# A two-block model on one core: masks of group 1, squares, mean square and evacuation of z at other places in the order of units

## The chip, the core and the metric

The program runs on one core of a Trainium2 chip. Its time is the device time of one execution in microseconds (us). TensorE multiplies matrices, VectorE and ScalarE work element by element, GpSimd (POOL in the profile) does a few small operations and issues some transfers, and SyncE (SP) issues nearly all transfers. Each engine works through its own queue in the order in which the program was written; between engines semaphores order the work.

## The reference, cut to what matters

256 tokens of width 2048 go through a state space layer, an attention layer, and a second block (neighbourhood attention and a large MLP). Only the state space layer is touched:

```python
def _mamba2_mixer(x, w_in, conv_w, conv_b, dt_bias, a_log, d_skip, norm_w, w_out):
    zxbcdt = x @ w_in                       # z 4096, xbc 6144, dt 64 columns
    xbc = silu(causal_conv4(xbc) + conv_b)  # xs 4096, B 8x128, C 8x128
    dt = softplus(dt_raw + dt_bias); a = -exp(a_log)
    y = _ssd_chunked(xs, dt, a, bm, cm) + xs * d_skip
    y = y * silu(z)
    yg = y.reshape(bsz, seqlen, 8, 512)
    yg = yg * rsqrt(mean(square(yg), axis=-1) + EPS)
    return (yg.reshape(...) * norm_w) @ w_out

# _ssd_chunked, for each head of a group (8 groups of 8 heads):
#   y[q] = sum over s <= q of (C[q] . B[s]) * exp(cum[q] - cum[s]) * dt[s] * x[s]
```

(`causal_conv4`, `silu`, `mean` and the comments stand for the reference's own longer lines.)

## The kernel before, in words

**Units.** The work of TensorE is a list of units, made by `plan` (from line 93). A unit multiplies one weight tile of 128 x 2048 (1 MB) with the activations. Every weight is split into a high part (`whi`, a copy in fp32r by ScalarE, L1399) and a low part (`wlo`, the rest, by VectorE, L1831), and so are the activations. A feature unit (form A) makes 128 output features for all 256 tokens, in one bank of PSUM: 16 matmuls of 512 columns (L1080) and 16 of 256 (L1084). A token unit (form B) makes 512 features for two tiles of 128 tokens, in two banks, 12 matmuls of 512 columns each (L1101, L1103, L1105). Banks 0 to 3 are taken in turn; a block waits until the one that was there four blocks before is evacuated. Banks 4 to 7, called `side[0]` to `side[3]`, serve all small work; `side_uses` (L651) names for every use which of them it takes, and a use waits until the use before it on that bank is read.

**The state space layer.** Group g has the units B, C, x0 to x3, then zf0 to zf3 (the gate z of that group), and then ao0 to ao3, the product of group g - 1 with the output weights. Group 0 has its z ahead instead and no ao behind it. So the units are 5 to 10 for group 0, 11 to 20 for B, C, x and z of group 1, 21 to 24 the output units of group 0, 25 to 34 group 2, 35 to 38 the output of group 1, and so on; 95 to 104 is group 7, 105 to 108 the output of group 6 and 109 to 112 that of group 7.

**The order within a unit** is written out by `script` (L222). For unit u: `late` of unit u - 1 (evacuation: of a feature unit, ScalarE copies the half with the low parts, L1446 for B, C and x and L1437 for z, and VectorE adds the other half, L1918 and L1899; for B, C and x the convolution follows on VectorE, L1791); `hi` and `lo` (split of the weights of unit u + 2); `post` (silu of unit u - 1 on ScalarE, L1453); what `timetable` put into `first`; the matmuls (of a token unit, the evacuation of its first block comes between its two halves); the load of the weights of unit u + 5; and what `timetable` put into `after`. Each engine runs those parts of this list that it has a part in, in this order.

**The group's own work** is the stage `ssd` with the steps n = 0, 1, 2, ..., one behind each unit from B of the group on (`timetable`, L162). `late = 2` in the names below is an offset for groups 0 and 1. The steps that the change touches or that stand beside them:
- `cb`: C·B for all pairs of tokens (TensorE, L1167 and L1168, into `side[2]`), and then the mask with the triangle on VectorE (L2049, "kcb"), at n = 3, for group 1 at n = 6;
- `px` at n = 7: x of the group transposed (TensorE, L1176, into `side[2]` and `side[3]`), then times dt (VectorE, L2058);
- the differences of the sums for the heads (Relu on ScalarE, L1512 and L1514), `decays`: Exp of them (L1552), times the mask (VectorE, L2066);
- `o` at n = 8 and 9 + late: the heads' products (TensorE, L1197 and L1199, `side[0]` and `side[1]`), then y1, y2 and y3 on VectorE (L2073, L2077, L2080): times exp(cum), plus the skip term (ScalarE, L1538, at n = 8), times silu(z);
- `sq` at n = 10 + late: the squares (ScalarE, L1542) and the high part of y times the norm's weight, `th` (L1546, into A2h);
- at n = 11 + late on VectorE two sums of the squares (L2083, L2085) and the low parts, `tl` (L1791 with A2l);
- `rs` at n = 12 + late: four products with a column of ones (TensorE, L1184, into `side[3]`);
- `ms` at n = 13 + late: scale and epsilon (VectorE, L2095), and the power -0.5 on GpSimd (L2502), which the evacuation of the group's output units needs (`mul_add` with SM);
- on SyncE: `cum_load` at n = 8 + late, the next group's sums broadcast to all partitions (1 MB, L957), and `exp_load` at n = 8, for group 1 at n = 9 (two of 256 KB, L968), behind `rs` of the group before.

The copies of z (L1437) wait until silu(z) of the group before has been used (`y3`, group - 1), since both share `zs`.

Of the kernel before, what the change touches and what calls it, by code (L numbers as in the profile page):

```python
# [16 lines left out]
NG = 8  # L17
# [146 lines left out]
def timetable(units):  # L164
    at = {u[1]: n for n, u in enumerate(units)}
# [7 lines left out]
    for g in range(NG):  # L173
        start = at["B", g]
        run(("ssd", g), start, 16 if g < 2 else 14)
        if g == 3:
            run(("rope",), at["C", 3], 7)
# [46 lines left out]
def script(units):  # L224
# [4 lines left out]
    for u, (form, tag, *_) in enumerate(units):  # L229
        to_pre = u < last and units[u + 1][1] in PRE  # L230
        if u:
            yield ("late", u - 1)
# [136 lines left out]
def stack_kernel(nc, wst, xT, xtok, pos, cols, rows, nabias, consts, out):  # L369
# [7 lines left out]
    with ExitStack() as ctx:  # L377
# [269 lines left out]
        def side_uses(s):  # L647
# [4 lines left out]
            elif what == "ssd":  # L652
                g, n = r
                late = 2 if g < 2 else 0
                if s == ("ssd", 0, 1):
                    yield from ((("zq", i), 2 + i) for i in range(2))
                if n == (6 if g == 1 else 3):
                    yield ("cb", g), 2
                if n == 7:
                    yield from ((("px", g, t), 2 + t) for t in range(NT))  # L660
                if n in (8 + late, 9 + late):
                    yield ("o", g, n - 8 - late), n - 8 - late
                if n == 12 + late:
                    yield ("rs", g), 3
            elif what == "turn":
# [228 lines left out]
        def sync_program(e):  # L894
# [75 lines left out]
            def ssd(g, n):  # L970
                late = 2 if g < 2 else 0
                if n == (9 if g == 1 else 8):
                    exp_load(g)
                if g == 0 and n == 3:
                    cum_load(0)
                if n == 8 + late and g + 1 < NG:
                    cum_load(g + 1)
# [66 lines left out]
        def tensor_program(e):  # L1044
# [106 lines left out]
            def ssd(g, n):  # L1151
                late = 2 if g < 2 else 0
                if g == 0 and n == 1:
                    w.wait_ge(s_ko, 16)
                    for i in range(2):
# [6 lines left out]
                        tr.then_inc(*ssd_p.inc(f"z{i}", 0))  # L1162
                if n == (6 if g == 1 else 3):
                    o = free(("cb", g))
                    w.wait_ge(*conv_a("silu", 6 * g))
                    w.wait_ge(*conv_a("silu", 6 * g + 1))
                    e.matmul(o[:, 0:T], xf[0][:, 0:P], xf[1], start=True, stop=True)  # L1167
                    e.matmul(o[:, T:T + P], xf[0][:, P:T], xf[1][:, P:T], start=True,  # L1168
                             stop=True).then_inc(*ssd_p.inc("cb", g))
# [8 lines left out]
                if n in (8 + late, 9 + late):  # L1178
                    heads_out(g, n - 8 - late)
                if n == 12 + late:  # L1180
                    o = free(("rs", g))
                    w.wait_ge(*ssd_v("a1", g))
                    for t in range(NT):
                        mean = e.matmul(o[:, t:t + 1], ex[:, t * P:(t + 1) * P], tri[:, P:P + 1], start=True, stop=True)  # L1184
                    mean.then_inc(*ssd_p.inc("rs", g))
# [182 lines left out]
        def scalar_program(e):  # L1368
# [133 lines left out]
            def ssd(g, n):  # L1502
# [25 lines left out]
                if n == 8:  # L1528
# [6 lines left out]
                    for f in range(4):  # L1535
# [3 lines left out]
                                     scale=CO[:, c:c + 1]).then_inc(*ssd_a.inc(f"k{f}", g))  # L1539
                if n == 10 + late:  # L1540
                    w.wait_ge(*ssd_v("y3", g))
# [245 lines left out]
        def vector_program(e):  # L1787
# [254 lines left out]
            def ssd(g, n):  # L2042
                late = 2 if g < 2 else 0
                if n == (6 if g == 1 else 3):
                    w.wait_ge(*ssd_p("cb", g))
# [28 lines left out]
                if n == 10 + late:  # L2074
# [5 lines left out]
                    e.tensor_tensor(yf, yf, zs, ALU.mult).then_inc(*ssd_v.inc("y3", g))  # L2080
                if n == 11 + late:
                    w.wait_ge(*ssd_a("sq", g))
# [5 lines left out]
                    for f in range(4):  # L2088
# [3 lines left out]
                                ALU.subtract).then_inc(*ssd_v.inc(f"tl{f}", g))  # L2092
                if n == 13 + late:
                    w.wait_ge(*ssd_p("rs", g))
                    e.tensor_scalar(SM[:, S_T + 2:S_T + 4], side[SIDE["rs", g][0]][:, 0:2], 1.0 / 512, EPS, ALU.mult,  # L2095
                                    ALU.add).then_inc(*ssd_v.inc("ms", g))
# [401 lines left out]
        def gpsimd_program(e):  # L2498
# [5 lines left out]
            def ssd(g, n):  # L2504
                if n == 13 + (2 if g < 2 else 0):
                    w.wait_ge(*ssd_v("ms", g))
# [175 lines left out]
```

## Time and profile before

| | us |
|---|---|
| median of 3 runs (2115.88 to 2117.52) | 2117.29 |
| the profiled execution | 2116.24 |
| its span | 2114.5 |
| TensorE busy (PE) | 2099.0, 99% |
| VectorE busy (DVE) | 1537.8, 73% |
| ScalarE busy (ACT) | 1133.1, 54% |
| GpSimd busy (POOL) | 53.6, 3% |
| mean granted clock of TensorE | 0.998 |

The span is from the first to the last instruction of the profiled execution. Busy times are sums over an engine's instructions; an engine can be busy and late at the same time, and its idle time costs only where TensorE, which ends last, waits for it. Times in the rows below are us from the start of the span, of this one execution. In a timeline a row merges neighbouring instructions of one line (xN is their number), and brackets give the idle time ahead of it and what ended it. PEclk is the granted clock as a share of full speed: 1.00 is 2.4 GHz, 0.50 is 1.2 GHz.

### The profile page before, as it was taken

To read this page: it belongs to the slowest core of one execution; us is meant where nothing else is said; L and a number is where in the kernel's file an instruction comes from. 1 tells how busy PE (TensorE), PEld (TensorE's weight loads), DVE (VectorE), ACT (ScalarE), POOL (GpSimd) and SP (SyncE) were. 2 spreads that over 40 slices of the span, in tenths; PEclk is the share of its full clock that TensorE was granted. 3 is DMA by queue.
4 is the path that set the end of the run, shared out by engine and by line. 5 is a ranking of instruction groups with operands and counts; after the bars stand their busy time and mean duration, and the time that the engine had idled before them with its cause. 6 is when DMAs were issued, how large, how long until landed. Compare 5 with 4: busy or idle time off the path is not lost.

```text
span 2114.5 us, 27498 instructions
## 1 busy us (share of the span) xinstructions
PE 2099.0 (99%) x10886; PEld 1773.8 (84%) x10886; DVE 1537.8 (73%) x2040; ACT 1133.1 (54%) x1411; POOL 53.6 (3%) x42
## 2 busy tenths in 40 slices
PE   9989999999999999999999999999999999999999
PEld 7878888888888888888888888888888888888887
DVE  7778778777778877675675556556778688787775
ACT  6765565665664556663555445544545454455452
POOL 0000000000000000000010111000000000000000
PEclk9999999999999999999999999999999999999999
DMA  8554555556555554445464544455575666556653
GB/s 320 202 201 170 209 187 201 190 194 210 192 199 181 196 192 146 156 142 199 168 241 174 192 173 161 172 184 201 197 239 183 221 211 197 224 186 212 239 177 141
DMA packets 68144, 411.28 MB, mean 195 GB/s; under 512 B 7472, under 2 KB 14384, under 8 KB 20656
## 3 DMA queue, kind: packets, MB, share of 16 engines
q1 hardware_dynamic: 66000, 394.85, 51.6%
q0 software_dynamic: 2016, 14.68, 3.8%
q8 instruction: 86, 1.41, 0.3%
q14 instruction: 42, 0.34, 0.0%
HBM read 407.27 MB, written 2.23 MB: 194 GB/s over the span
## 4 chain that ended last, share of the span: by engine, by line
PE 91%; DVE 2%; ACT 1%; issue 1%; DMA 0%; POOL 0%; SPq 0%; DVEq 0%
PE bank L1080 23%; PE bank L1101 15%; PE bank L1105 14%; PE bank L1103 14%; PE bank L1084 12%; PE bank L1117 2%; PE bank L1119 2%; PE bank L1121 2%; PE bank L1335 1%; DVE wlo L1831 1%; PE bank L1271 1%; PE bank L1197 1%; PE bank L1293 0%; PE bank L1230 0%; PE bank L1323 0%
## 5 line engine op out<-in xcount | busy, mean ns | idle before, releaser
L1831 DVE TENSOR_TENSOR wlo<-raw,whi 128x2048 fp32r<-128x2048 f32 x318 | 727.8, 2289 | 259.0 <-ACT whi L1399 228.7
L1399 ACT ACTIVATE whi<-raw 128x2048 fp32r<-128x2048 f32 x318 | 607.1, 1911 | 262.1 <-PE bank L1105 246.7
L1080 PE MATMUL bank<-A,whi 128*128 128x512 f32 x2448 | 590.7, 394 | 0.0
L1080 PEld LDWEIGHTS bank<-A,whi 128*128 128x128 f32 x2448 | 454.0, 189 | 93.1 <-issue 2.4
L1084 PEld LDWEIGHTS bank<-A,wlo 128*128 128x128 f32 x2448 | 313.9, 191 | 11.9
L1084 PE MATMUL bank<-A,wlo 128*128 128x256 f32 x2448 | 317.4, 283 | 0.0
L1101 PE MATMUL bank<-whi,A2h 128*128 128x512 f32 x800 | 314.2, 393 | 0.0
L1103 PE MATMUL bank<-whi,A2l 128*128 128x512 f32 x800 | 311.7, 390 | 0.0
L1105 PE MATMUL bank<-wlo,A2h 128*128 128x512 f32 x800 | 311.5, 389 | 0.0
L1101 PE MATMUL bank<-whi,A 128*128 128x512 f32 x608 | 241.9, 398 | 0.8 <-ACT whi L1389 0.8
L1105 PE MATMUL bank<-wlo,A 128*128 128x512 f32 x608 | 237.7, 391 | 0.1
L1103 PE MATMUL bank<-whi,A 128*128 128x512 f32 x608 | 237.1, 390 | 0.0
L1101 PEld LDWEIGHTS bank<-whi,A2h 128*128 128x128 f32 x800 | 150.2, 188 | 32.1 <-issue 1.4
L1105 PEld LDWEIGHTS bank<-wlo,A2h 128*128 128x128 f32 x800 | 150.2, 188 | 31.7
L1103 PEld LDWEIGHTS bank<-whi,A2l 128*128 128x128 f32 x800 | 150.3, 188 | 30.4
L1831 DVE TENSOR_TENSOR wlo<-W,whi 128x2048 fp32r<-128x2048 f32 x56 | 128.3, 2291 | 45.4 <-ACT whi L1399 44.6
L1399 ACT ACTIVATE whi<-W 128x2048 fp32r<-128x2048 f32 x56 | 107.0, 1914 | 68.9 <-DVE W L1842 45.7
L1105 PEld LDWEIGHTS bank<-wlo,A 128*128 128x128 f32 x608 | 114.1, 188 | 26.6 <-DVE wlo L1819 2.7
L1101 PEld LDWEIGHTS bank<-whi,A 128*128 128x128 f32 x608 | 114.3, 188 | 25.5 <-issue 1.7
L1103 PEld LDWEIGHTS bank<-whi,A 128*128 128x128 f32 x608 | 114.3, 188 | 23.1 <-DVE A L2208 0.7
L1434 ACT ACTIVATE W<-bank 128x256 f32<-128x256 f32 x60 | 23.0, 384 | 180.4 <-PE bank L1084 180.4
L1791 DVE SCALAR_TENSOR_TENSOR XR<-bank,SM,XR 128x512 f32<-128x512 f32 x110 | 80.8, 746 | 16.4 <-PE bank L1105 16.3
(262 smaller groups left out, 1831.4 us busy)
## 6 DMA issues: line engine op xcount, KB each, us to landing
raw<-wst SPq DMA_DIRECT2D x313, 1024.0 KB, 4.8
W<-wst SPq DMA_DIRECT2D x33, 1024.0 KB, 5.0
W<-wst POOLq DMA_DIRECT2D x9, 1024.0 KB, 8.0
W<-cum_scratch SPq DMA_DIRECT2D x8, 1024.0 KB, 8.2
W<-rows SPq DMA_DIRECT2D x21, 256.0 KB, 5.8
raw<-wst POOLq DMA_DIRECT2D x5, 1024.0 KB, 7.9
raw<-wst SPq DMA_DIRECT2D x16, 256.0 KB, 7.3
W<-exp_scratch SPq DMA_DIRECT2D x16, 256.0 KB, 6.4
```

Source lines behind the costliest of these rows:

```text
L1080: e.matmul(o[:, :], whi[:, s, k * P:(k + 1) * P], A1[:, k, :, :].rearrange("p h t -> p (h t)"), start=k == 0, stop=False)
L1084: last = e.matmul(o[:, T:2 * T], wlo[:, s, k * P:(k + 1) * P], A1h[:, k, :], start=False, stop=k == KT - 1)
L1101: e.matmul(o, h, wh, start=opens and k == 0, stop=False)
L1103: e.matmul(o, low, wh, start=False, stop=False)
L1105: last = e.matmul(o, h, wl, start=False, stop=t in shut(tag) and k == 3)
L1117: e.matmul(o, h, wh, start=name in ("a", "b", "d", "f") and k == 0, stop=False)
L1119: e.matmul(o, low, wh, start=False, stop=False)
L1121: last = e.matmul(o, h, wl, start=False, stop=k == 3)
L1399: e.activation(whi[:, u % 3, :], raw_of(u), ACT.Copy).then_inc(*hi.inc((u, 3)))
L1434: e.activation(W[:, M_R + i % 4 * T:M_R + (i % 4 + 1) * T], rest, ACT.Copy).then_inc(*rest_a.inc(u))
L1791: return e.scalar_tensor_tensor(out=o, in0=a, scalar=s, in1=b, op0=op0, op1=op1)
L1831: e.tensor_tensor(wlo[:, u % 3, :], raw_of(u), whi[:, u % 3, :], ALU.subtract).then_inc(*lo.inc((u, 3)))
```

## The change

The stage `ssd` keeps its operations and sizes; their places in the list move.
- Group 1's `cb` (products and masks) is at n = 4 instead of 6, that is after unit 15 instead of after unit 17.
- For all groups, squares and `th` are at 11 + late (before 10), the sums and `tl` at 12 + late (11), `rs` at 13 + late (12), `ms` and the power at 14 + late (13): one unit later each. `rs` takes `side[1]` instead of `side[3]`.
- Because of the added step, groups 0 and 7, whose steps fill all units up to their first output unit, get the last one in `first` of that output unit (21 and 109).
- `exp_load` is at n = 10 for group 1 (9) and at n = 6 for all others (8).
- The z units of group 1: `late` of units 17 and 18 is dropped from its place in units 18 and 19 and stands, ahead of `late` of unit 19, at the head of unit 20.

```diff
--- before.py
+++ after.py
@@ -172,7 +172,12 @@
     run(("dt",), at["z", 0, 3], 8)
     for g in range(NG):
         start = at["B", g]
-        run(("ssd", g), start, 16 if g < 2 else 14)
+        if g in (0, NG - 1):
+            steps = at["ao", g, 0] - start
+            run(("ssd", g), start, steps)
+            first[at["ao", g, 0]].append(("ssd", g, steps))
+        else:
+            run(("ssd", g), start, 17 if g == 1 else 15)
         if g == 3:
             run(("rope",), at["C", 3], 7)
     q0 = at["q", 0, 0]
@@ -228,7 +233,9 @@
     yield ("begin",)
     for u, (form, tag, *_) in enumerate(units):
         to_pre = u < last and units[u + 1][1] in PRE
-        if u:
+        if tag == ("zf", 1, 3):
+            yield from (("late", u - 3), ("late", u - 2))
+        if u and tag not in (("zf", 1, 1), ("zf", 1, 2)):
             yield ("late", u - 1)
         if tag in PRE:
             r = PRE[tag]
@@ -654,14 +661,14 @@
                 late = 2 if g < 2 else 0
                 if s == ("ssd", 0, 1):
                     yield from ((("zq", i), 2 + i) for i in range(2))
-                if n == (6 if g == 1 else 3):
+                if n == (4 if g == 1 else 3):
                     yield ("cb", g), 2
                 if n == 7:
                     yield from ((("px", g, t), 2 + t) for t in range(NT))
                 if n in (8 + late, 9 + late):
                     yield ("o", g, n - 8 - late), n - 8 - late
-                if n == 12 + late:
-                    yield ("rs", g), 3
+                if n == 13 + late:
+                    yield ("rs", g), 1
             elif what == "turn":
                 yield from ((("turn", r[0], r[1], pr), 2 * r[1] + pr) for pr in range(2))
             elif what == "quarter":
@@ -969,7 +976,7 @@
 
             def ssd(g, n):
                 late = 2 if g < 2 else 0
-                if n == (9 if g == 1 else 8):
+                if n == (10 if g == 1 else 6):
                     exp_load(g)
                 if g == 0 and n == 3:
                     cum_load(0)
@@ -1160,7 +1167,7 @@
                                 tr = e.transpose(o[:, f * T + t * P:f * T + (t + 1) * P],
                                                  z0[t][:, (2 * i + f) * P:(2 * i + f + 1) * P], ident)
                         tr.then_inc(*ssd_p.inc(f"z{i}", 0))
-                if n == (6 if g == 1 else 3):
+                if n == (4 if g == 1 else 3):
                     o = free(("cb", g))
                     w.wait_ge(*conv_a("silu", 6 * g))
                     w.wait_ge(*conv_a("silu", 6 * g + 1))
@@ -1177,7 +1184,7 @@
                     tr.then_inc(*ssd_p.inc("px", g))
                 if n in (8 + late, 9 + late):
                     heads_out(g, n - 8 - late)
-                if n == 12 + late:
+                if n == 13 + late:
                     o = free(("rs", g))
                     w.wait_ge(*ssd_v("a1", g))
                     for t in range(NT):
@@ -1537,7 +1544,7 @@
                         w.wait_ge(*conv_a("silu", 6 * g + 2 + f))
                         e.activation(yf[:, f, :], xf[2 + f], ACT.Identity,
                                      scale=CO[:, c:c + 1]).then_inc(*ssd_a.inc(f"k{f}", g))
-                if n == 10 + late:
+                if n == 11 + late:
                     w.wait_ge(*ssd_v("y3", g))
                     e.activation(ex, y, ACT.Square).then_inc(*ssd_a.inc("sq", g))
                     if g >= 2:
@@ -2041,7 +2048,7 @@
 
             def ssd(g, n):
                 late = 2 if g < 2 else 0
-                if n == (6 if g == 1 else 3):
+                if n == (4 if g == 1 else 3):
                     w.wait_ge(*ssd_p("cb", g))
                     w.wait_ge(s_ko, 16)
                     if g:
@@ -2078,7 +2085,7 @@
                     w.wait_ge(*ssd_v("y2", g))
                     w.wait_ge(*(zs_a("s", g) if g else ssd_a("zs1", 0)))
                     e.tensor_tensor(yf, yf, zs, ALU.mult).then_inc(*ssd_v.inc("y3", g))
-                if n == 11 + late:
+                if n == 12 + late:
                     w.wait_ge(*ssd_a("sq", g))
                     e.tensor_tensor(ex[:, 0:512], ex[:, 0:512], ex[:, 512:1024], ALU.add).then_inc(*ssd_v.inc("a0", g))
                     w.wait_ge(*ssd_v("a0", g))
@@ -2090,7 +2097,7 @@
                         w.wait_ge(*ssd_a(f"th{f}", g))
                         mul_add(A2l[:, kt, :], yf[:, f, :], norm_w(g, f), A2h[:, kt, :], ALU.mult,
                                 ALU.subtract).then_inc(*ssd_v.inc(f"tl{f}", g))
-                if n == 13 + late:
+                if n == 14 + late:
                     w.wait_ge(*ssd_p("rs", g))
                     e.tensor_scalar(SM[:, S_T + 2:S_T + 4], side[SIDE["rs", g][0]][:, 0:2], 1.0 / 512, EPS, ALU.mult,
                                     ALU.add).then_inc(*ssd_v.inc("ms", g))
@@ -2502,7 +2509,7 @@
                 return e.tensor_tensor(SM[:, to:to + n], SM[:, src:src + n], SM[:, S_MH:S_MH + n], ALU.pow)
 
             def ssd(g, n):
-                if n == 13 + (2 if g < 2 else 0):
+                if n == 14 + (2 if g < 2 else 0):
                     w.wait_ge(*ssd_v("ms", g))
                     if g >= 2:
                         w.wait_ge(*evac_v((at["ao", g - 2, ND - 1], 1)))
```

## Rows read from the trace of the kernel before

**Rows 1.** What TensorE waited for, 0 to 700 us: us, times, longest.

```profile
PE bank L1184 <- DVE W L2058: 4.3, 1, 4.3
PE bank L1176 <- DVE W L2049: 3.3, 1, 3.3
PE bank L1184 <- DVE W L2085: 0.7, 1, 0.7
```

**Rows 2.** TensorE's timeline: start us, us, what [idle before <-releaser].

```profile
82.64 1.04 PE L1176 MATMUL bank<-KO,W 128*128 128x128 f32 x8
...
83.43 3.92 PE L1080 MATMUL bank<-A,whi 128*128 128x512 f32 x16
...
124.42 1.52 PE L1176 MATMUL bank<-KO,W 128*128 128x128 f32 x8 [3.30 <-DVE W L2049]
...
137.03 1.02 PE L1184 MATMUL bank<-KO,W 128*128 128x1 f32 x4 [4.34 <-DVE W L2058]
...
145.47 0.40 PE L1101 MATMUL bank<-whi,A2h 128*128 128x512 f32 x1
...
151.03 0.65 PE L1197 MATMUL bank<-W 128*64 128x256 f32 x4
...
158.14 0.65 PE L1197 MATMUL bank<-W 128*64 128x256 f32 x4
```

**Rows 3.** Windows: us, busy of PE, PEld, DVE, ACT, POOL; PEclk; DMA.

```profile
126.00:128.00 2.00, 2.00 (x6) 1.52 (x6) 0.00 (x0) 2.00 (x7) 0.00 (x0) 0.50 0.00 0
...
139.00:141.00 2.00, 2.00 (x6) 1.55 (x5) 2.00 (x2) 2.00 (x7) 0.00 (x0) 0.50 0.07 16
```

**Rows 4.** VectorE's timeline in the same stretch.

```profile
122.68 1.23 DVE L2080 TENSOR_TENSOR W<-W 128x1024 f32<-128x1024 f32 x1
...
123.82 0.55 DVE L2049 TENSOR_TENSOR W<-bank,KO 128x384 f32<-128x384 f32 x1
...
129.03 0.42 DVE L1899 TENSOR_TENSOR W<-bank,W 128x256 f32<-128x256 f32 x1 [4.66 <-ACT W L1437]
...
133.04 0.69 DVE L2083 TENSOR_TENSOR W<-W 128x512 f32<-128x512 f32 x1
...
134.11 1.66 DVE L1791 SCALAR_TENSOR_TENSOR A2l<-W,CO,A2h 128x256 fp32r<-128x256 f32 x4
...
139.42 1.75 DVE L2066 TENSOR_TENSOR W<-W 128x1536 f32<-128x1536 f32 x1
```

**Rows 5.** ScalarE's timeline in the same stretch.

```profile
123.94 1.06 ACT L1542 ACTIVATE W<-W 128x1024 f32<-128x1024 f32 x1 [4.90 <-DVE W L2080]
...
124.90 1.69 ACT L1546 ACTIVATE A2h<-W,CO 128x256 fp32r<-128x256 f32 x4
...
126.50 0.49 ACT L1512 ACTIVATE W<-W 128x256 f32<-128x256 f32 x1
...
128.83 1.90 ACT L1399 ACTIVATE whi<-raw 128x2048 fp32r<-128x2048 f32 x1
...
136.27 1.28 ACT L1552 ACT_TABLE_LOAD   x1
...
138.96 1.69 ACT L1538 ACTIVATE W<-W,CO 128x256 f32<-128x256 f32 x4
...
140.56 0.36 ACT L1437 ACTIVATE W<-bank 128x256 f32<-128x256 f32 x1
```

**Rows 6.** GpSimd's timeline, 100 to 170 us.

```profile
145.34 2.10 POOL L2502 TENSOR_TENSOR SM<-SM 128x2 f32<-128x2 f32 x1 [144.89 <-DVE SM L2095]
```

**Rows 7.** Broadcasts: sums (by tile), wait before L2073, exp (page).

```profile
L957 SPq DMA_DIRECT2D W<-cum_scratch x1: 423/423/423, 111.6 to 111.6; - x1
DMA to landing us min/median/max: 7.0/7.0/7.0
...
  DMA W<-exp_scratch: 17.9, 6
...
W<-exp_scratch SPq DMA_DIRECT2D x16, 256.0 KB, 6.4
```

## The prediction

> **What bounds the kernel now.** The first view is the list of what TensorE waited for: the reader is to see that, apart from startup and the norms, only three rows name the state space layer, 4.3, 3.3 and 0.7 us [rows 1]. TensorE sets the end of this program, so only what it waits for, or does at a lower clock, can be won. The second view is TensorE's timeline around the two long waits [rows 2]. It shows that unit 18 ends at 124.42 - 3.30 = 121.1, that the transposes of x of group 1 then stand for the masks (L2049), that the mean square of group 0 stands from 132.7 to 137.0 for L2058, and that unit 21, the first output unit, opens at 145.47. A whole unit takes 151.03 - 145.47 = 5.56 us at full clock (a feature unit has the same number of columns, 12288), the eight transposes 83.43 - 82.64 = 0.79. So the waits cost more than their length: from 124.42 to 132.69 is 8.27 us for 0.79 + 5.56 = 6.35, 1.9 too long, and from 137.03 to 145.47 is 8.44 for 5.56 and four one-column products, which is 2.9 too long with the products at nothing and 1.9 with them at their 1.02 us. The third view, the windows, says why: the granted clock is 0.50 (1.2 GHz) in both stretches after TensorE had stood [rows 3]. The two waits cost 3.3 + 1.9 + 4.3 + about 2.4 = 11.9 us together. The fourth and fifth views are the queues of VectorE and ScalarE in the same stretch [rows 4, 5]: both run several units behind and are busy in a chain, so their order decides.
>
> **The waits that go.** Masks of group 1: the C·B products go from after unit 17 to after unit 15, and VectorE's masks with them. Their inputs were made long before, and the bank side[2] of the transposes is then free at about 111.5 instead of 124.3. TensorE's products only change place (no gain, no loss before unit 18). The transposes start at 121.1, 3.3 us sooner, provided that silu of x is ready; ScalarE has nothing left before 123.94 - 4.90 = 119.0 [rows 5], so it is. Mean square of group 0: it is now a unit later and on side[1], whose last reader is y1 of group 0, so the bank of the px transposes (4.3 us) isn't waited for. The mean square one unit later also has the 0.7 us wait of group 3 behind it: squares, sums and products all move by one unit, but the squares no longer hold up ScalarE's and VectorE's splits, and a unit is 5.56 us. I take all 0.7 (bounds: nothing, and 1.1 with its clock).
>
> **What is late next.** The dropped `late` steps put the evacuations of z units 17, 18 and 19 behind one another at the head of unit 20. They run on ScalarE (the copy) and then on VectorE (the add), and unit 21 needs the banks of units 17 and 18 (units 17 to 20 hold the four banks, and its two blocks take the next two in turn). I follow the queues.
> The product with silu(z) of group 0 (L2080) ended at 122.68 + 1.23 = 123.9; the 0.5 us of the masks now stand ahead of it, so 124.4 [rows 4]. ScalarE meanwhile does the Relu rows of heads 0 to 2 and the split of unit 20: the broadcast of the sums was issued at 111.6 and landed in 7.0 us, 118.6 [rows 7], so 119.5 + 2.1 + 1.9 = 123.5, in time.
> From 124.4 on ScalarE has: squares 0.96 (123.94 to 124.90), the four products with the norm's weight 1.60 (to 126.50), three heads of Relu 2.1 (2.33 to the split at 128.83, with a copy of 0.36, partly overlapped, that now isn't there), the split of unit 21 1.90: 130.9. Then two heads 1.4, the table for Exp and Exp 2.69 (136.27 to 138.96): 135.0. Then the skip products (L1538), which wait for VectorE's last A2l [rows 5].
> VectorE: low part of unit 21 from 131.0, 2.29 less overlap: 133.2; two sums of squares 1.07 (133.04 to 134.11): 134.3; four A2l 1.66: 135.9; decay of heads 0 to 3 (L2066) 1.75 to 137.6 [rows 4].
> So the skip products run from 135.9 for 1.60 to 137.5, the copy of unit 17 takes 0.36 to 137.9, the add 0.42 (as at 129.03) to 138.4, and unit 21 opens at 138.5.
> TensorE: transposes 121.1 to 121.9, unit 19 to 127.5, unit 20 to 133.0 (its halves are ready at 123.5 and 126.7). There it waits 1.3 us for the sums (134.3), does the mean square, under 0.5, and waits 3.7 us more for the bank. In 5.5 us it has nearly nothing to do, more than in either of the old gaps, so I charge the clock as those do: 1.9 and 1.9 to 2.9 were lost, I take 2.2, and as bounds 0 (the idle time comes in two pieces, and each might be too short) and 2.9.
>
> Here the Trainium skill speaks against me a little. The table load shows as 1.28 us, and from its start to the instruction behind Exp (1.48) are only 2.69 [rows 5]. The Trainium skill (ScalarE: Activation LUTs, section What ACT_TABLE_LOAD costs) adds to it a drain of some 1380 ns at each change of table. Beside Exp there is no room for it. By the page Exp would end at 136.4 and unit 21 open at about 139.0; the gain would be 0.5 us smaller.
>
> **The sum.** Unit 21 opens at 138.5 instead of 145.47: 7.0 us sooner. The lower clock, which was over there before, now falls into unit 21: -2.2. That leaves 4.8, and with the 0.7 of group 3, 5.5 us. The profiled execution took 2116.24 us (span 2114.5, 1.7 us around it) and would be 2110.7; the median of the runs is 2117.29, 1.05 above it, so I forecast 2117.29 - 5.5 = 2111.8 us.
>
> **Edits that I cost at nothing.** The scaling of group 0 (`ms`) now stands in `first` of unit 21, behind the late part and the split of unit 23, and GpSimd's power behind it took 2.10 us the first time [rows 6]. VectorE: add of unit 19 at 139.3, low of unit 22 at 142.6 (high from 138.6), decay 144.3, add of unit 20 144.7, low of unit 23 146.9, scale 147.0, GpSimd until 149.2, evacuation of the first output block 149.9. VectorE stands 2 us for it. Its cover is TensorE itself: unit 21 lasts until 146.3, head products and unit 22 take 158.14 - 151.03 = 7.1 [rows 2], to 153.4, the next head products 1.5, so unit 23 needs that bank at 154.9. Margin 5 us; each us beyond it costs one.
> The load of exp: two issues. For groups 2 to 7 two units sooner, and this ends most of VectorE's 17.9 us of waiting for it [rows 7], which hid behind TensorE anyway; on SP's queue they pass two weight loads, whose tiles are needed three units on. For group 1 it is one unit later, behind the load of unit 26: issued near 147.3, landed after 6.4 at about 154.3 with its second half, VectorE ready for it at 153.6: under 1 us of VectorE, none of TensorE. For group 0 sooner, nothing waits for it.
> Group 7: its scale now stands in `first` of unit 109, before the evacuation of that unit. VectorE waits there for one power; the banks of unit 111 are two units off. Nothing to 0.3 us.
> Squares one unit later in groups 2 to 6: the output units that use them are ten units off.
>
> **Rivals.** *The wait really goes.* If unit 17's bank were free when TensorE arrives, unit 21 would open at 133.5 without a loss of clock: 12.0 + 0.7 = 12.7 us, 2104.6. For it: both named rows vanish. Against: the chain above is 4.9 us too long, and only if ScalarE's copies stood before its Relu rows would it be cut. My own case with the clock kept (7.0 + 0.7 = 7.7 us, 2109.6) is no part of this one.
> *The new wait is longer than worked out.* The chain on ScalarE has no slack; 1.5 to 4 us more in it (the broadcast lands later than 118.6, or ScalarE and VectorE wait for each other once more) leave a gain of 1.5 to 4: about 2114.5, no change that can be measured. For it: the chain is followed in both queues. Against: each duration has a row and the steps repeat to 0.1 us.
> *Given back at unit 23, slower.* One mechanism: the scale of group 0 is behind the low part of unit 23 and the 2.10 us power, and VectorE, in order, stands at the evacuation with everything behind it. It decides once that evacuation ends after 154.9, that is 5 us later than worked out; 5.5 us more eat the gain, and with the lower clock again (2.2) the time is about 2120. For it: VectorE really stands there, where it didn't before. Against: 5 us of margin.
>
> **How the numbers follow.** Differences under 0.2% (4.2 us) can't be told from no change here. My case 0.64, with its own range 2109.0 to 2113.5 (clock loss 0 to 2.9, opening within 0.8 us); 0.04 of it lies under 4.2 us. The wait goes: 0.12. Longer wait: 0.18, all within 0.2%. Slower: 0.06. So faster 0.60 + 0.12 = 0.72, same 0.04 + 0.18 = 0.22, slower 0.06. The range 2106.0 to 2115.0 holds my case and nearly all of the third, and leaves out the first rival (0.12) and the slower one (0.06), less than 2 in 10.
>
> **What would show it.** Right: L1176 and L1184 no longer wait for L2049 and L2058; a wait of 3 to 4 us appears at the first L1101 of unit 21, released by L1899, behind one of about 1 us at L1184 for L2085; the granted clock is 0.50 for some us at that place and nowhere else in the layer; unit 22 starts about 5 us sooner; POOL's first power now comes behind the split of unit 23, with a VectorE wait for it; L2073 hardly waits for exp. Wrong: unit 21 opens before 136 or after 140, a wait of TensorE at unit 23, or one between 660 and 690 us that was not there.

## The result, and the profile after

The changed kernel takes 2110.93 us (median of 9 runs, 2109.32 to 2112.02), the kernel before on the same chip 2116.47 (9 runs). The ratio is 0.9973, 95% interval 0.9962 to 0.9983: 5.5 us, or 0.27%, faster. The forecast was 5.5 us faster, as a time 2111.8 us, worked out from the 2117.29 of the first three runs of the kernel before.

The profiled execution took 2109.32 us (that of before: 2116.24). Lines of the new kernel stand 7 further down: L1087 is what L1080 was, L1183 the transposes, L1191 the mean square, L1906 the add of z.

```profile
span 2107.5 us, 27512 instructions
...
PE 2096.1 (99%) x10886; PEld 1771.5 (84%) x10886; DVE 1539.2 (73%) x2040; ACT 1135.2 (54%) x1411; POOL 52.3 (2%) x42
```

What TensorE waited for, 0 to 700 us (us, times, longest):

```profile
PE bank L1108 <- DVE W L1906: 3.4, 1, 3.4
PE bank L1191 <- DVE W L2092: 1.5, 1, 1.5
PE bank L1064 <- DVE SM L1802: 1.3, 1, 1.3
PE bank L1216 <- DVE XR L2197: 0.8, 2, 0.6
```

The three rows of before [rows 1] are gone. In their place stand two: 1.5 us at the mean square (L1191) for the sums (L2092), and 3.4 us at the first matmul of unit 21 (L1108) for the add of z unit 17 (L1906). The rest is startup (L1064) and the norm (L1216).

TensorE's timeline (start us, us, what, idle before and releaser), which answers to [rows 2]:

```profile
120.02 1.03 PE L1183 MATMUL bank<-KO,W 128*128 128x128 f32 x8
...
133.71 0.58 PE L1191 MATMUL bank<-KO,W 128*128 128x1 f32 x4 [1.53 <-DVE W L2092]
137.72 0.80 PE L1108 MATMUL bank<-whi,A2h 128*128 128x512 f32 x1 [3.44 <-DVE W L1906]
...
145.02 0.65 PE L1204 MATMUL bank<-W 128*64 128x256 f32 x4
```

The transposes follow unit 18 without a wait, at 120.0. Unit 21 opens at 137.72 and lasts until 145.02: 7.30 us where 5.56 are needed. In the windows (us; busy of PE, PEld, DVE, ACT, POOL; granted clock; DMA) the reader sees why, as in [rows 3]:

```profile
138.00:140.00 2.00, 2.00 (x5) 1.54 (x6) 0.68 (x2) 2.00 (x2) 0.00 (x0) 0.50 0.00 0
...
142.00:144.00 2.00, 2.00 (x10) 1.66 (x9) 2.00 (x3) 1.98 (x2) 0.00 (x0) 1.00 0.40 82
```

The clock is at its lower level, 0.50 (1.2 GHz), for the first part of unit 21 and back at 1.00 from 142. This execution was 1.1 us ahead of that of before already when unit 18 ended (120.02 against 121.12). That is startup: both wait 1.3 us for VectorE's first constants, and before shows two more waits of 0.8 us in all for the first split weights; in the thirteen profiles of this study the end of unit 18 lies between 120.0 and 121.5 us. So a fairer measure of the stretch is from the end of unit 18 to the head products behind unit 21: 151.03 - 121.12 = 29.9 us before, 145.02 - 120.02 = 25.0 after. The profiled spans differ by 7.0 us: 4.9 in this stretch, 1.1 at startup, 0.7 at group 3's mean square, and 0.3 elsewhere. At full clock and without a wait the stretch would be 0.8 + 3 x 5.56 + 0.4 = 17.9.

This measure scatters too, because the chain on VectorE and ScalarE doesn't keep step with TensorE. In the nine profiles that have both the moved steps and the early masks, and so the same work up to that point, the product with silu(z) (L2087) ends between 2.6 and 4.3 us after unit 18 (3.5 with the change). So two stretches in which TensorE waits for this chain can differ by up to 1.7 us through that alone.

VectorE's timeline in this stretch, which answers to [rows 4]:

```profile
110.17 0.55 DVE L2056 TENSOR_TENSOR W<-bank,KO 128x384 f32<-128x384 f32 x1
...
130.21 2.29 DVE L1838 TENSOR_TENSOR wlo<-raw,whi 128x2048 fp32r<-128x2048 f32 x1 [3.28 <-issue]
132.42 0.68 DVE L2090 TENSOR_TENSOR W<-W 128x512 f32<-128x512 f32 x1
133.13 0.42 DVE L2092 TENSOR_TENSOR W<-W 128x256 f32<-128x256 f32 x1
...
137.24 1.09 DVE L1906 TENSOR_TENSOR W<-bank,W 128x256 f32<-128x256 f32 x3 [0.42 <-ACT W L1444]
...
146.05 0.15 DVE L2102 TENSOR_SCALAR SM<-bank 128x2 f32<-128x2 f32 x1
147.22 1.41 DVE L1798 SCALAR_TENSOR_TENSOR XR<-bank,SM,XR 128x512 f32<-128x512 f32 x2 [1.01 <-POOL SM L2509]
...
154.18 0.69 DVE L2080 TENSOR_TENSOR W<-bank,W 128x512 f32<-128x512 f32 x1 [2.69 <-DMA W<-exp_scratch]
```

The masks (L2056) stand at 110.2, ahead of the evacuations of x. The low part of unit 21 comes at 130.2 behind 3.28 us of idleness, and only then the two sums, to 133.6. At 137.24 the three z blocks are added in one go. And ScalarE's [rows 5]:

```profile
123.56 1.06 ACT L1549 ACTIVATE W<-W 128x1024 f32<-128x1024 f32 x1 [1.01 <-DVE W L2087]
...
131.52 1.28 ACT L1559 ACT_TABLE_LOAD   x1
132.82 1.49 ACT L1559 ACTIVATE W<-W 128x1536 f32<-128x1536 f32 x1
135.23 1.71 ACT L1545 ACTIVATE W<-W,CO 128x256 f32<-128x256 f32 x4 [0.93 <-issue]
136.84 0.90 ACT L1444 ACTIVATE W<-bank 128x256 f32<-128x256 f32 x3
```

Its chain runs from the squares through the heads' Relus and the splits (not shown) to the table, Exp, the skip products (L1545, 0.93 us late, behind VectorE's A2l) and then the three copies (L1444).

### The profile page after: what moved, and what is told of

It reads as the page before. It is cut to its first block, busy times and chain, and to the rows that moved or that the text cites. A ratio compares the mean times of both kernels' runs of the same rounds, so it can differ in the third digit from the quotient of the medians.

```text
span 2107.5 us, 27512 instructions
## 1 busy us (share of the span) xinstructions
PE 2096.1 (99%) x10886; PEld 1771.5 (84%) x10886; DVE 1539.2 (73%) x2040; ACT 1135.2 (54%) x1411; POOL 52.3 (2%) x42
## 4 chain that ended last, share of the span: by engine, by line
PE 93%; DVE 1%; ACT 0%; POOL 0%; issue 0%; DVEq 0%
PE bank L1087 24%; PE bank L1108 15%; PE bank L1112 15%; PE bank L1110 15%; PE bank L1091 12%; PE bank L1124 2%; PE bank L1126 2%; PE bank L1128 2%; PE bank L1204 1%; PE bank L1342 1%; PE bank L1278 1%; PE bank L1300 0%; PE bank L1237 0%; PE bank L1330 0%; PE bank L1355 0%; PE bank L1311 0%
## 5 line engine op out<-in xcount | busy, mean ns | idle before, releaser
L1087 PE MATMUL bank<-A,whi 128*128 128x512 f32 x2448 | 587.7, 392 | 0.0
L1087 PEld LDWEIGHTS bank<-A,whi 128*128 128x128 f32 x2448 | 451.1, 188 | 91.7 <-issue 2.2
L1108 PE MATMUL bank<-whi,A2h 128*128 128x512 f32 x800 | 314.6, 393 | 3.4 <-DVE W L1906 3.4
L1108 PE MATMUL bank<-whi,A 128*128 128x512 f32 x608 | 241.8, 398 | 0.0
L1108 PEld LDWEIGHTS bank<-whi,A2h 128*128 128x128 f32 x800 | 150.6, 188 | 36.0 <-DVE W L1906 3.5
L1108 PEld LDWEIGHTS bank<-whi,A 128*128 128x128 f32 x608 | 114.2, 188 | 24.6 <-issue 1.7
```

Of the source, the lines that this page charges most:

```text
L1087: e.matmul(o[:, :], whi[:, s, k * P:(k + 1) * P], A1[:, k, :, :].rearrange("p h t -> p (h t)"), start=k == 0, stop=False)
L1108: e.matmul(o, h, wh, start=opens and k == 0, stop=False)
```

## The experiments

Each ran beside the kernel before on the same chip, the first four on one, the next three on a second and the last four on a third; so kernels of different groups are compared by their ratios to the kernel before. "Stretch" is the time from the end of unit 18 to the head products behind unit 21 in its profile: 29.9 us before, 25.0 with the change.

**The masks alone.** The kernel before with one edit, at all three places:

```diff
-if n == (6 if g == 1 else 3):
+if n == (4 if g == 1 else 3):
```

> The kernel before with one edit: C.B and masks of group 1 at n = 4 instead of 6. Theory of queues (the squares, sums and A2l of group 0 run in a chain on ScalarE and VectorE that doesn't wait for TensorE): the 3.3 us wait at L1176 goes, but the mean square product of group 0, which stands behind VectorE's L2058 at the end of that chain, starts where it did, near 137.5; its wait grows from 4.3 to about 10 us, unit 21 opens at 145.5 to 146, and the time is that of before within 1 us. Rival (each wait is worth its length and the lower clock behind it): 3.3 + 1.9 = 5.2 us faster.

Measured: 2117.93 us against 2117.19, ratio 1.0002 (0.9994 to 1.0011). TensorE and VectorE:

```profile
120.85 1.04 PE L1176 MATMUL bank<-KO,W 128*128 128x128 f32 x8
...
138.29 1.01 PE L1184 MATMUL bank<-KO,W 128*128 128x1 f32 x4 [10.86 <-DVE W L2058]
...
152.70 0.65 PE L1197 MATMUL bank<-W 128*64 128x256 f32 x4
```

```profile
134.31 0.69 DVE L2083 TENSOR_TENSOR W<-W 128x512 f32<-128x512 f32 x1
...
136.95 1.28 DVE L2058 TENSOR_TENSOR W<-bank,W 128x512 f32<-128x512 f32 x2
```

The transposes start without a wait, and TensorE then stands 10.9 us for L2058 instead of 4.3. VectorE's sums (L2083) come when the chain lets them, whatever TensorE does; here 1.3 us later than before, 0.5 of them because the masks now stand ahead of the chain. The other 0.8 stood before the masks already, at the decay (L2066, 105.60 for 104.79). Unit 21 opens at 147.14, later than the 145.5 to 146 expected, and the stretch is 31.9, 2.0 longer than before; the medians are 0.7 us apart, which is no difference. The early masks take away a wait and bring nothing. The rival, 5.2 us faster, falls.

**The steps alone.** The changed kernel with `cb` at n = 6 for group 1 and `late` of every unit at its own place:

```diff
-        if tag == ("zf", 1, 3):
-            yield from (("late", u - 3), ("late", u - 2))
-        if u and tag not in (("zf", 1, 1), ("zf", 1, 2)):
+        if u:
             yield ("late", u - 1)
```

> The changed kernel without the early masks and without the bunched z evacuations: only the steps of squares, sums, mean square, scale and the exp loads moved. Theory of queues: transposes still wait 3.3 us for L2049 and unit 19 runs 1.9 us long, unit 20 ends at 138.2, by then the sums (136.4) and A2l (137.9) are made and unit 21 opens near 138.7 at full clock, 5.6 us long. That is 7 to 7.5 us faster than before and 1 to 2 us faster than the whole change. Rival (the parts add up, the masks' wait is paid on top): 5.2 us slower than the whole change, about as before.

Measured: 2108.97 us against 2117.19, ratio 0.9958 (0.9946 to 0.9971).

```profile
124.41 1.97 PE L1181 MATMUL bank<-KO,W 128*128 128x128 f32 x8 [3.63 <-DVE W L2054]
...
138.06 0.50 PE L1189 MATMUL bank<-KO,W 128*128 128x1 f32 x4
...
144.08 0.65 PE L1202 MATMUL bank<-W 128*64 128x256 f32 x4
```

The masks' wait is paid (3.6 us, and the first transposes and matmuls at the lower clock), but unit 20 then ends at 138.06, when sums and A2l are ready, and unit 21 runs 5.66 us. Stretch 23.3, 1.7 less than with the whole change. The moved steps (with the exp loads and the mean square's new bank) give all the gain. That the other two parts together take 1.7 us away isn't shown: the intervals of the two ratios overlap, and the stretch with the change scatters by as much.

One rival within this part was not tried. The mean square's step and its bank, `side[1]` for `side[3]`, were always moved together. The kernel before has these two rows:

```profile
133.76 0.42 DVE L2085 TENSOR_TENSOR W<-W 128x256 f32<-128x256 f32 x1
...
135.69 1.28 DVE L2058 TENSOR_TENSOR W<-bank,W 128x512 f32<-128x512 f32 x2
```

The sums end at 134.2 and the reading of the old bank at 137.0. By this estimate the new bank alone, at the old step, would shorten the 4.3 us wait by 2.8 us. How much of the gain is the bank's and how much the step's stays open.

**The change without the bunched evacuation** (of the whole change, only the edit of `late` just shown is taken back):

> The changed kernel with the z evacuations of group 1 back at their own places. Theory of queues: ScalarE takes the copy of unit 17 at 124.4 ahead of the split of unit 20, everything behind is 2.5 us later, so the mean square waits for the sums until about 136.8 (3.7 us), unit 21 opens at about 137.6 to 138.4 with the lower clock: within 1 us of the whole change. The wait for the bank (L1906) is gone and replaced by one on L2092. Rival (the bunched evacuation is the whole new wait): 3.4 to 5 us faster than the whole change.

Measured: 2109.55 us against 2117.19, ratio 0.9962 (0.9948 to 0.9975).

```profile
137.17 0.99 PE L1189 MATMUL bank<-KO,W 128*128 128x1 f32 x4 [3.92 <-DVE W L2090]
138.01 0.77 PE L1106 MATMUL bank<-whi,A2h 128*128 128x512 f32 x1
...
146.04 0.65 PE L1202 MATMUL bank<-W 128*64 128x256 f32 x4
```

The wait for L1906 is gone, and 3.9 us for the sums stand before it. Stretch 24.9, as with the whole change: bunching moved the wait behind the mean square, no more. Unit 21 lasts 8.0 us here, 0.7 more than with the change.

**The change without the early masks** (`cb` back at n = 6 for group 1):

> The changed kernel with the C.B products and masks of group 1 back at n = 6. Theory of queues: transposes wait 3.3 us for L2049, unit 19 is 1.9 us long, unit 20 ends at 138.2 and unit 21 opens at 138.6, no later than in the whole change, since its bank (unit 17) is free at 138; no wait of 3.4 us there, so full clock in unit 21: about 2 us faster than the whole change. Rival (the early masks bring what they take away): 3.3 to 5.2 us slower than the whole change.

Measured: 2108.23 us against 2117.19, ratio 0.9958 (0.9946 to 0.9971).

```profile
123.92 1.97 PE L1183 MATMUL bank<-KO,W 128*128 128x128 f32 x8 [3.20 <-DVE W L2056]
...
137.62 0.50 PE L1191 MATMUL bank<-KO,W 128*128 128x1 f32 x4
...
143.64 0.65 PE L1204 MATMUL bank<-W 128*64 128x256 f32 x4
```

TensorE stands 3.2 us once, early, and finds bank, sums and A2l ready at 138. Stretch 22.9, 2.1 less than the whole change, as expected. The ratios' intervals overlap, so that the masks are better late is likely and not shown; that taking them back costs 3.3 to 5.2 us, the rival, is ruled out.

**Two evacuations at unit 19.** The change with the copies and adds of z units 17 and 18 ahead of unit 21's split:

```diff
-        if tag == ("zf", 1, 3):
-            yield from (("late", u - 3), ("late", u - 2))
-        if u and tag not in (("zf", 1, 1), ("zf", 1, 2)):
+        if tag == ("zf", 1, 2):
+            yield ("late", u - 2)
+        if u and tag != ("zf", 1, 1):
             yield ("late", u - 1)
```

> The changed kernel, but the evacuations of z units 17 and 18 stand at the head of unit 19 instead of unit 20 (that of unit 19 at its usual place in unit 20). Theory of queues: ScalarE's two copies (0.6 us) then run before its split of unit 21 and VectorE's adds in its idle time before 130, so the bank of unit 17 is long free; the mean square waits until about 135.0 for the sums and unit 21 opens at about 136.0 for A2l, 2.5 us sooner than worked out for the whole change. TensorE stands 2.5 to 3 us instead of 5 in all; if the clock falls all the same the gain over the whole change is 2 to 2.5 us, if it holds 4 to 4.5 us. Rival (ScalarE's chain as a whole is the limit, not the place of the copies): unit 21 opens where it did, no gain.

Measured: 2107.17 us against 2116.16, ratio 0.9959 (0.9947 to 0.9972).

```profile
134.41 0.82 PE L1191 MATMUL bank<-KO,W 128*128 128x1 f32 x4 [1.88 <-DVE W L2092]
135.08 0.77 PE L1108 MATMUL bank<-whi,A2h 128*128 128x512 f32 x1
...
142.10 0.65 PE L1204 MATMUL bank<-W 128*64 128x256 f32 x4
```

The wait for the bank is gone and that for the sums is 1.9 us; unit 21 opens 14.7 us behind the end of unit 18 (17.7 with the change). The clock still fell, so unit 21 lasts 7.0 us. Stretch 21.7, 3.3 less than the change, more than the 2 to 2.5 expected for a clock that falls; unit 21 had been expected at 136.0 and opens at 135.08.

**Matmuls in the wait.** The change with extra matmuls on constants behind group 0's mean square, twelve calls:

```diff
                     mean.then_inc(*ssd_p.inc("rs", g))
+                    if g == 0:
+                        w.wait_ge(*ssd_v("xd1", 1))
+                        for _ in range(12):
+                            e.matmul(side[3][:, 0:T], KO[:, 0:P], KO[:, 0:T], start=True, stop=True)
```

> The changed kernel with 12 extra matmuls of 256 columns on constants (about 0.23 us each, 2.8 us) behind the mean square of group 0, where TensorE stands 3.4 us for the bank. Their results are never read. Theory (the lower clock in unit 21 comes from TensorE standing before it): the granted clock stays at 1.00, unit 21 takes 5.6 us instead of 7.3, the program is 1.7 us faster. Rival (the clock falls from the first gap of 1.5 us or for another reason): the extra matmuls run at half clock, and the time is the same or up to 2 us longer.

Measured: 2112.18 us against 2116.16, ratio 0.9980 (0.9971 to 0.9988). Each call ran as two matmuls of 0.21 us, 5.1 us in all, so the fill itself held unit 21 until 139.2; unit 21 then took 5.8 us at full clock (stretch 24.1). This is not the 1.7 us gain that was expected. Its 11 runs lie between 2109.39 and 2114.76, wider than the others, and the profiled one is the lowest. Their mean granted clocks go with their times: 1.000 in the four up to 2110.51, 0.999 in the three from 2111.30 to 2112.54, 0.998 in the four from 2113.35 on. A mean lower by 0.002 over 2107 us is 4.2 us lost, as an estimate, if TensorE works all through the slower time, and the times differ by about as much. So the clock stayed up in some executions and not in others; where it was lost in the slower ones no profile shows. The same kernel was made with seven calls (`range(7)`), to end before the bank is free:

> The changed kernel with 7 extra matmul calls instead of 12 behind the mean square of group 0 (each ran as two of 0.21 us, so 3.0 us in all, against a wait of 3.4 us). Results never read. Theory (the clock falls because TensorE stands): the fill ends before the bank is free, unit 21 opens where it did in the changed kernel and takes 5.6 to 5.8 us instead of 7.3: 1.5 to 1.7 us faster than the changed kernel. Rival (the lower clock isn't worth its time, because the queues behind limit): the same time.

Measured: 2108.74 us against 2117.49, ratio 0.9966 (0.9953 to 0.9978). Timeline and one window:

```profile
135.16 3.27 PE L1196 MATMUL bank<-KO 128*128 128x256 f32 x14
138.72 0.50 PE L1108 MATMUL bank<-whi,A2h 128*128 128x512 f32 x1 [0.29 <-DVE W L1910]
...
144.39 0.65 PE L1208 MATMUL bank<-W 128*64 128x256 f32 x4
```

```profile
138.00:140.00 2.00, 1.71 (x8) 1.08 (x8) 1.09 (x3) 2.00 (x4) 0.00 (x0) 1.00 0.11 41
```

Unit 21 takes 5.67 us at a granted clock of 1.00 instead of 7.30: the lower clock is what costs the 1.7 us, and with matmuls in the wait it can stay up. Here the sums were 0.6 us later than with the change, counted from unit 18, and the fill ended just before the bank was free (a wait of 0.29 is left), so the stretch is 24.0, only 1.0 less than the change, and the interval holds the changed kernel's ratio too. Of its five runs three have a mean clock of 1.000, one 0.999, and the slowest, 2112.70, 0.998. No run of the change or of the kernel with the old exp loads, 16 together, reached 1.000. The clock's price is shown in the profile, not by the median.

**The exp loads back at their old steps:**

```diff
-                if n == (10 if g == 1 else 6):
+                if n == (9 if g == 1 else 8):
                     exp_load(g)
```

> The changed kernel with the exp loads back at their old steps (n = 9 for group 1, 8 for the others). Theory: VectorE waits again for exp in groups 2 to 7 (17.9 us in all), hidden behind TensorE; the time is that of the whole change within 0.5 us. Rival (part of the gain, or the 0.7 us wait of group 3, comes from the earlier loads): 0.7 to 1.5 us slower.

Measured: 2109.76 us, ratio 0.9970 (0.9958 to 0.9981), by 0.0003 that of the change (0.9973). VectorE's idle time ahead of L2080 (us, times):

```profile
  DMA W<-exp_scratch: 18.6, 6
```

VectorE waited 18.6 us again (2.7 with the change, once, in group 1), and none of it reached TensorE.

**The sums one step sooner.** The change with VectorE's sums and A2l of group 0 in the step of the squares:

```diff
-                if n == 12 + late:
+                if n == 12 + late - (g == 0):
                     w.wait_ge(*ssd_a("sq", g))
```

> The changed kernel with VectorE's sums of squares and A2l of group 0 one step sooner (after unit 18, in the step of the squares themselves, where VectorE stood idle from 126.9 to 130.2). The z evacuations stay bunched at unit 20. Theory of queues: sums are ready at about 128, so the 1.5 us wait of the mean square goes; ScalarE's skip products start at Exp's end, 134.2 instead of 135.2, so the bank of unit 17 is free near 136.8 and unit 21 opens there, about 0.9 us sooner than in the changed kernel, behind a single wait of about 4.4 us and with the lower clock: 0.9 us faster than the changed kernel. Rival (the sums were the limit): 4 us or more faster.

Measured: 2109.36 us against 2117.49, ratio 0.9967 (0.9954 to 0.9979).

```profile
133.44 0.50 PE L1191 MATMUL bank<-KO,W 128*128 128x1 f32 x4
138.90 0.80 PE L1108 MATMUL bank<-whi,A2h 128*128 128x512 f32 x1 [4.96 <-DVE W L1906]
...
145.95 0.65 PE L1204 MATMUL bank<-W 128*64 128x256 f32 x4
```

The mean square waits for nothing, and the bank is waited for 5.0 us instead. Stretch 24.5, half a us less than the change; but here L2087 ends 0.8 us later behind unit 18, and counted from its end unit 21 opens 1.1 us sooner (13.1 us for 14.2), near the 0.9 expected.

**Both.** The last edit and the two evacuations at unit 19 together:

> The last kernel, and z units 17 and 18 evacuated at the head of unit 19 as in the kernel with two at 19. Theory of queues: neither sums nor bank are late any more; TensorE goes from unit 20 through the mean square into unit 21 without a wait, at about 132.5 in the changed kernel's time (137.7 there), at full clock. 5.2 + 1.7 = 6.9 us at that place; up to 1 us is given back at unit 22 (VectorE's split, ready near 140) or at unit 23 (its bank waits for the scale and GpSimd's power, near 146). So 5.5 to 7 us faster than the changed kernel, about 12 us faster than before. Rival (a third wait of the same size stands behind the two): 3 us or less faster than the changed kernel.

Measured: 2104.03 us against 2117.49, ratio 0.9940 (0.9926 to 0.9953). Its interval lies wholly below that of the changed kernel. The timeline, with the one wait left in the stretch:

```profile
120.24 1.04 PE L1183 MATMUL bank<-KO,W 128*128 128x128 f32 x8
...
132.24 0.50 PE L1191 MATMUL bank<-KO,W 128*128 128x1 f32 x4
132.60 0.48 PE L1108 MATMUL bank<-whi,A2h 128*128 128x512 f32 x1
...
134.03 0.50 PE L1112 MATMUL bank<-wlo,A2h 128*128 128x512 f32 x1 [0.72 <-DVE wlo L1838]
...
139.24 0.65 PE L1204 MATMUL bank<-W 128*64 128x256 f32 x4
```

Unit 21 opens 0.36 us behind the start of the mean square, at full clock. Stretch 19.0, 6.0 less than the change, as expected (5.5 to 7). What is above the possible 17.9 is mostly the wait of 0.7 us for VectorE's low part of unit 21, the third bound behind the two; unit 22, behind the stretch, waits 0.5 us for its own.

**Both, and the scale of group 0 one step sooner** (the same edit on VectorE and GpSimd):

```diff
-                if n == 14 + late:
+                if n == 14 + late - (g == 0):
                     w.wait_ge(*ssd_p("rs", g))
```

> The last kernel with scale and power of group 0 one step sooner, behind unit 20. Theory: VectorE no longer stands for GpSimd before the evacuation of unit 21's first block, so a wait of TensorE at unit 23 would go; the scale must now wait for the mean square on VectorE, which is long done when VectorE gets there. 0 to 1 us faster than the last kernel. Rival: VectorE meets the mean square too soon and is itself held up: 0 to 1 us slower.

Measured: 2103.84 us against 2117.49, ratio 0.9940 (0.9927 to 0.9952): no difference.

```profile
135.17 0.50 PE L1112 MATMUL bank<-wlo,A2h 128*128 128x512 f32 x1 [0.64 <-DVE wlo L1838]
```

There was no wait at unit 23 to be taken away; TensorE waits for the low parts of units 21 and 22 as in the last kernel (1.1 us together for 1.2), and the stretch is 18.9.

## Why the prediction was right

- *Masks.* The transposes start at once, and the bank is free at 110.17 + 0.55 = 110.7 (111.5 was worked out; less the 1.1 us of startup, 110.4). Right. The prediction priced their wait as won; the first experiment shows that its going brings nothing unless the chain behind it is shortened too. In the sum the wrong price did no harm, because the sum was made from the opening of unit 21 and not from the waits' lengths.
- *The chain on ScalarE and VectorE.* Worked out: unit 21 opens 17.4 us after the end of unit 18 (138.5 - 121.1). Measured: 137.72 - 120.02 = 17.7. The two waits were forecast at 1.3 and 3.7 us and are 1.5 and 3.4. Right, and by the named releasers. The 0.3 us are less than the chain scatters by from one execution to the next.
- *The clock.* 2.2 us were charged, 1.74 measured. It fell at this place, and nowhere else in the layer (1.00 from 20 to 100 us and from 160 to 700). The bound 0 was wrong: with 1.5 + 3.4 us of waits, and even with 1.9 (two evacuations at unit 19), the clock fell.
- *The table.* The Trainium skill (ScalarE: Activation LUTs, section What ACT_TABLE_LOAD costs) would have Exp start 1.4 us later than the load's end; it started at 132.82, 1.30 after the start of the load at 131.52, which itself takes 1.28. There is no room ahead of the load either: the Relu before it ended at 131.51. The trace doesn't agree with the page, and the half us was rightly left out.
- *Scale and power behind unit 23's split.* VectorE stood for it, 1.01 us instead of 2. The power took 0.72 us, not the 2.10 of [rows 6]:

```profile
146.36 0.72 POOL L2509 TENSOR_TENSOR SM<-SM 128x2 f32<-128x2 f32 x1 [145.91 <-DVE SM L2102]
```

  TensorE didn't wait at unit 23, and the earlier scale gained nothing: the slower rival had no ground.
- *Group 3.* Its 0.7 us are gone, as in the steps alone, while the masks alone still have waits at L2085.
- *Exp loads.* Nothing for TensorE, as said. In group 1 VectorE stood 2.7 us for exp, not under 1. Counted from the end of unit 18, it came to L2080 after 31.5 us where 32.5 were worked out, mostly since the power was 1.4 us shorter, and exp was there after 34.2, not 33.2: its second load was issued at 147.2, and the two took 6.4 and 6.9 us to land.
- *The size.* The stretch gave 4.9 us (forecast 4.8), group 3 0.7. Within the stretch two errors cancel: unit 21 opened 6.6 us sooner behind unit 18, not 7.0, and the clock cost 1.7, not 2.2. With the scatter of the chain this makes the agreement of the medians to 0.1 us luck; what the runs bear out is the mechanism and a size of some us.
- *The rival that the wait really goes* priced 12.7 us. It didn't come true, since the bank stayed late as worked out. But this is what the two evacuations at 19 and the early sums together reach: 13.5 us by the medians, 10.9 in the stretch.

## What to carry to other kernels

Follow the in-order queues of the engines that feed the bottleneck and price a change by when the next needed thing is ready, not by the length of the wait that it removes: a removed wait of 3.3 us with its clock brought nothing, and leaving it in did no harm. Where two things are late behind one another (here the sums and a bank), moving one lets the other show: the sums sooner gave about 1 us or less, the bank sooner 3.3 of the stretch, both 6.0. When work is put off, put it off to a place ahead of the next long chain and into the other engine's idle time.

## What the runs showed of the hardware

TensorE's granted clock fell to 0.50 after waits of 1.9, 3.2 and 10.9 us alike, and the loss in the unit behind didn't follow the length of the wait. A unit of 5.56 us at full clock lasted 7.0 us behind 1.9 us (two evacuations at unit 19), 7.3 behind 1.5 and 3.4 (the change), 8.0 behind 3.9 (no bunch), 7.05 behind 5.0 (sums one step sooner) and 8.0 behind 10.9 (masks alone).

Nor does the length alone decide whether it falls. With two evacuations at unit 19 TensorE took up work at 134.41 after 1.88 us; the clock was 0.98 until 134.6 and 0.50 from there, so it fell while TensorE was working again. With seven calls in the wait TensorE had stood 2.15 us before the mean square, and the clock stayed at 1.00. Matmuls whose results nobody reads kept the clock up in both profiles that have them, but by the mean clocks of the single runs in only some of the executions (1.000 in 7 of 16).

GpSimd's first power took 2.10 us in the profile of before, 2.09 with the masks alone and 2.09 with the scale one step sooner, and 0.72 in the ten others. In those three it stands behind unit 20, in the others at the head of unit 21. So its place in the list goes with the 1.4 us; by what mechanism isn't shown.
